# Forgetting attention: weights by values as two passes of rounded operands and rests, the dense group cut in halves between them

## The reference, cut to what matters

```python
def attend(q_blk, c_blk, q_pos):
    s = jnp.einsum('bqhd,bkhd->bhqk', q_blk, k)
    s = s + c_blk[..., None] - c[:, :, None, :]
    s = jnp.where(q_pos[:, None] >= key_pos[None, :], s, -jnp.inf)
    p = jax.nn.softmax(s, axis=-1)
    return jnp.einsum('bhqk,bkhd->bqhd', p.astype(v.dtype), v)
...
o = o * jax.nn.sigmoid(o_gate)
return o @ w_out
```

## Time and profile before

| | us |
|---|---|
| median of 3 runs | 2766.43 |
| lowest and highest of them | 2764.67, 2767.55 |
| the profiled execution | 2765.52 |
| its span, first to last instruction | 2763.8 |
| TensorE busy in the span | 2699.0 (98%) |
| VectorE busy | 1820.4 (66%) |
| ScalarE busy | 1366.1 (49%) |

### The profile page before, as it was taken

How to read it: one execution, slowest core, us unless ns; L and a number is a source line. 1 busy time by engine, 2 the same in 40 slices (tenths; PEclk the granted TensorE clock), 3 DMA queues, 4 the chain that set the end, 5 groups by cost and what they waited for, 6 DMA issues and landing times.

```text
span 2763.8 us, 50228 instructions
## 1 busy us (share of the span) xinstructions
PE 2699.0 (98%) x18315; PEld 2455.7 (89%) x18315; DVE 1820.4 (66%) x2928; ACT 1366.1 (49%) x2401; POOL 307.5 (11%) x269
## 2 busy tenths in 40 slices
PE   7999999999989999899999999999999999899998
PEld 6898899999989999899988888887899988699986
DVE  6777757886367766678853453553677775588832
ACT  4455445664245554556642223232488884455632
POOL 2000011330022121023201011010000000000000
PEclk9999999999999999999999999999999999999999
DMA  4232226884331111268833222223312222223332
GB/s 127 69 76 58 60 75 131 175 181 106 92 97 54 53 53 46 80 144 178 169 105 113 84 72 83 87 68 88 92 54 61 61 61 84 76 85 106 108 94 73
DMA packets 458590, 254.24 MB, mean 92 GB/s; under 512 B 9222, under 2 KB 452871, under 8 KB 458359
## 3 DMA queue, kind: packets, MB, share of 16 engines
q1 hardware_dynamic: 414550, 211.45, 27.0%
q0 software_dynamic: 43152, 38.63, 7.7%
q10 hardware_dynamic: 784, 2.75, 0.3%
HBM read 250.67 MB, written 2.13 MB: 91 GB/s over the span
## 4 chain that ended last, share of the span: by engine, by line
PE 55%; DVE 6%; DMA 4%; issue 3%; ACT 2%; POOL 1%; POOLq 0%; DVEq 0%; ACTq 0%
PE ps L525 24%; PE ps L529 14%; PE ps L919 7%; PE ps L1110 2%; DMA w_sum1a<-in_ffn_w_gate 2%; DMA w_sum1b<-in_ffn_w_gate 2%; PE ps L1268 2%; PE ps L1309 1%; DVE wl L492 1%; PE ps L1298 1%; PE ps L1330 1%; PE ps L1235 1%; PE ps L1155 1%; PE ps L1221 0%; ACT wh L488 0%
## 5 line engine op out<-in xcount | busy, mean ns | idle before, releaser
L492 DVE TENSOR_TENSOR wl<-raw,wh 128x1024 fp32r<-128x1024 f32 (+3 forms) x312 | 370.6, 1188 | 298.3 <-ACT wh L488 295.6
L488 ACT ACTIVATE wh<-raw 128x1024 fp32r<-128x1024 f32 (+3 forms) x312 | 307.0, 986 | 386.5 <-PE ps L525 217.3
L529 PE MATMUL ps<-xh,wh 128*128 128x264 f32 x1872 | 393.6, 291 | 11.3 <-DVE xl L559 6.7
L529 PE MATMUL ps<-xl,wh 128*128 128x264 f32 x1872 | 381.9, 285 | 0.0
L529 PE MATMUL ps<-xh,wl 128*128 128x264 f32 x1872 | 381.6, 285 | 0.0
L529 PEld LDWEIGHTS ps<-xh,wh 128*128 128x128 f32 x1872 | 292.5, 189 | 20.8 <-issue 10.5
L529 PEld LDWEIGHTS ps<-xl,wh 128*128 128x128 f32 x1872 | 291.5, 189 | 0.0
L529 PEld LDWEIGHTS ps<-xh,wl 128*128 128x128 f32 x1872 | 290.6, 189 | 0.0
L525 PE MATMUL ps<-xh,wh 128*128 128x512 f32 x528 | 213.5, 404 | 2.3 <-DVE wl L492 2.3
L525 PE MATMUL ps<-xl,wh 128*128 128x512 f32 x528 | 208.9, 396 | 0.0
L525 PE MATMUL ps<-xh,wl 128*128 128x512 f32 x528 | 207.7, 393 | 0.0
(11 more groups left out here) (453 smaller groups left out, 6603.0 us busy)
## 6 DMA issues: line engine op xcount, KB each, us to landing
raw<-in_w_in SPq DMA_DIRECT2D x88, 512.0 KB, 3.9
raw<-in_ffn_w_gate SPq DMA_DIRECT2D x44, 512.0 KB, 5.6
raw<-in_ffn_w_up SPq DMA_DIRECT2D x44, 512.0 KB, 5.0
raw<-in_w_ffn_in SPq DMA_DIRECT2D x44, 512.0 KB, 3.8
raw<-in_fox_w_in SPq DMA_DIRECT2D x33, 512.0 KB, 4.2
raw<-in_hgrn_w_in SPq DMA_DIRECT2D x32, 512.0 KB, 4.0
raw<-in_ffn_w_down SPq DMA_DIRECT2D x32, 448.0 KB, 3.7
raw<-in_ffn_w_up POOLq DMA_DIRECT2D x36, 256.0 KB, 6.9
```

The lines of the kernel that those rows point to most:

```text
L488: nc.scalar.activation(wh[:, v % 2, 0:nk, :], raw[:, v % RAW_SLOTS, 0:nk, :], ACT.Copy).then_inc(s("w_hi"), 1)
L492: nc.vector.tensor_tensor(wl[:, v % 2, 0:nk, :], raw[:, v % RAW_SLOTS, 0:nk, :], wh[:, v % 2, 0:nk, :].bitcast(F32), ALU.subtract).then_in ...
L529: last = nc.tensor.matmul(ps[:, bank + b, 0:HALF], w[:, slot, kk, :], x[:, k0 + k, b * HALF:(b + 1) * HALF], start=first, stop=end_)
```

## The change

`fox_out` works on fp32r operands. The values become `v_p`: for each head 64 columns rounded and 64 columns of rests side by side, so that one stationary tile of 128 columns holds both (the rounded part first for head 0, the rest first for head 1). The weights become `p_h` (rounded) and `p_l` (rests), and every strip is streamed twice, once from each. So the half of bank 5 where the rounded values stand receives their product and the other half that of the rests, and the two halves have to be added afterwards: ACT copies the other half into `o_t` (`shift`), DVE adds the own half to it (`add_halves`), and the same for the 16 last tokens (`shift_tails`, `add_tails`).

The parts are made by both engines: ACT copies the rounded values and all strips of the rounded weights out of PSUM, DVE subtracts them from PSUM for the rests (`value_rest`, `weight_rest`). The banks may be written again only when DVE is done with them too, so `scores` of head 0 now also waits for `value_rest`. Dense group 3 is cut in two: its first half stays between `turned(0)` and `fox_out(0)`, its second goes behind `turned(1)`. `fox_sums` is cut in two: the queries' sums stand before the second half, the keys' sums behind `fox_out(1)`. The gate's logits, its exponential and its reciprocal move behind with group 3. In the last pair the same value and weight work runs, and the dense work between is as before.

```diff
-    p_t = a.take("p_t", [P, N_STRIP])
-    v_t = a.take("v_t", [P, NTT, P])
+    p_h = a.take("p_h", [P, N_STRIP], F32R)
+    v_p = a.take("v_p", [P, NTT, 4, FOX_D], F32R)
...
+    p_l = a.take("p_l", [P, N_STRIP], F32R)
...
         def fox_out(i, b):
-            pe.wait_ge(s("pt_a"), 2 * i + b + 1)
-            pe.wait_ge(s("pt_b"), 2 * i + b + 1)
-            lo, hi = FOX_D * b, FOX_D * (b + 1)
-            causal_pv(lambda t: ps[lo:hi, 5, t:SEQ], ps[lo:hi, 4, 496:512],
-                      lambda j, k: v_t[0:k, j, lo:hi], p_t, FOX_D).then_inc(s("o_mm"), 1)
+
+            for n, (p, ready) in enumerate(((p_h, "pv_act"), (p_l, "pv_dve"))):
+                pe.wait_ge(s(ready), 10 * i + 4 * b + 4)
+                if b and not n:
+                    pe.wait_ge(s("pv_dve"), 10 * i + 5)
+                for j in range(NFULL):
+                    nc.tensor.matmul(ps[:, 5, P * j:SEQ], v_p[:, j, 2 * b:2 * b + 2, :].rearrange("p b n -> p (b n)"),
+                                     p[:, STRIP0[j]:STRIP0[j] + SEQ - P * j], start=(n + j == 0), stop=(n == 1 and j == NFULL - 1))
...
-            pe.wait_ge(s("vt_ready"), i + 1)
+            pe.wait_ge(s("pv_act"), 10 * i + 1)
+            pe.wait_ge(s("pv_dve"), 10 * i + 1)
             pe.wait_ge(s("o_done"), i + 1)
...
             turned(0)
             if ahead_:
-                pe_group(pe, PH_FOX, i, 3, xh, xl)
+                pe_group(pe, PH_FOX, i, 3, xh, xl, part=0)
...
             turned(1)
             if ahead_:
-                pe.wait_ge(s("psum_free"), evacuated(PH_FOX, i, 3))
-                fox_sums(i + 1)
+                pe.wait_ge(s("psum_free"), evacuated(PH_FOX, i, 2))
+                fox_sums(i + 1, 0)
+                pe_group(pe, PH_FOX, i, 3, xh, xl, part=1)
             else:
                 out_tiles(0, 6, 7)
             fox_out(i, 1)
+            if ahead_:
+                pe.wait_ge(s("psum_free"), evacuated(PH_FOX, i, 3))
+                fox_sums(i + 1, 1)
...
+            def value_rest():
+                dve.wait_ge(s("pv_act"), 10 * i + 1)
+                V.tensor_tensor(v_p[:, 0:NFULL, 1:3, :], ps[:, 2, :].rearrange("p (j b n) -> p j b n", j=NFULL, b=2),
+                                v_p[:, 0:NFULL, 0:4:3, :].bitcast(F32), ALU.subtract)
...
+            def weight_rest(b):
+                for n in range(2):
+                    dve.wait_ge(s("pv_act"), 10 * i + 4 * b + n + 2)
+                    V.tensor_tensor(p_l[:, 512 * n:512 * (n + 1)], ps[:, 2 + n, :], p_h[:, 512 * n:512 * (n + 1)].bitcast(F32),
+                                    ALU.subtract).then_inc(s("pv_dve"), 1)
...
             if ahead_:
                 split_ahead(dve, dve_lo, PH_FOX, i, 0)
+                value_rest()
...
                 scaled_out(PH_FOX, i, 2, v_s[:, :])
-                evacuate(0)
+                weight_rest(0)
                 split_ahead(dve, dve_lo, PH_FOX, i, 3)
-                scaled_out(PH_FOX, i, 3, g_s[:, :])
...
-            gate()
-            evacuate(1)
+                gate()
+            add_halves(0)
+            weight_rest(1)
             if ahead_:
                 qk_scaled(i + 1, 0)
+                scaled_out(PH_FOX, i, 3, g_s[:, :])
                 query_parts(i + 1)
+                gate()
+            add_halves(1)
+            add_tails()
+            if ahead_:
                 qk_scaled(i + 1, 1)
```

More of the change, by code:

```diff
@@ L845, in _ @@
         sp.wait_ge(s("stored"), 16 * NFULL)
[L848 to L857, removed]
     def transposes(src, bank, rows_=P):
@@ L965, in feed_forward, with fox_sums @@
             dense(down, *hidden, ("hid_ready", FT * n))
[L968 to L975, removed]
+        def fox_sums(n, j):
+            pe.wait_ge(s("qn_sq"), 2 * n + j + 1)
+            for b in range(2):
+                last = nc.tensor.matmul(ps[:, FOX_BANKS[j] + b, 0:HALF], mean_64, sq[:, j, b * HALF:(b + 1) * HALF],
+                                        start=True, stop=True)
+            last.then_inc(s("qn_sum"), 1)
         def scores(i, b):
@@ L1008, in fox_out @@
         def fox_out(i, b):
-            pe.wait_ge(s("pt_a"), 2 * i + b + 1)
-            pe.wait_ge(s("pt_b"), 2 * i + b + 1)
-            lo, hi = FOX_D * b, FOX_D * (b + 1)
-            causal_pv(lambda t: ps[lo:hi, 5, t:SEQ], ps[lo:hi, 4, 496:512],
-                      lambda j, k: v_t[0:k, j, lo:hi], p_t, FOX_D).then_inc(s("o_mm"), 1)
+            for n, (p, ready) in enumerate(((p_h, "pv_act"), (p_l, "pv_dve"))):
[5 more added lines that the diff above has]
+                                     p[:, STRIP0[j]:STRIP0[j] + SEQ - P * j], start=(n + j == 0), stop=(n == 1 and j == NFULL - 1))
+            for n, p in enumerate((p_h, p_l)):
+                for j in range(NTT):
+                    k = TOK[j]
+                    last = nc.tensor.matmul(ps[:, 4, tail_out(b)], v_p[0:k, j, 2 * b:2 * b + 2, :].rearrange("p b n -> p (b n)"),
+                                            p[0:k, tail_at(j):tail_at(j) + TAIL], start=(n + j == 0), stop=(n == 1 and j == NFULL))
+            last.then_inc(s("o_mm"), 1)
         def pair_(i, ahead_):
@@ L1073, in _ @@
         pe.wait_ge(s("psum_free"), evacuated(PH_FOXP, 0, 3))
-        fox_sums(0)
+        for j in range(2):
+            fox_sums(0, j)
         loop(pe, PH_FOX.n, lambda i: pair_(i, True))
@@ L1718, in qk_square, with qk_rsqrt @@
             nc.scalar.activation(sq[:, j, :], qk_raw[:, j, :], ACT.Square).then_inc(s("qn_sq"), 1)
-        def qk_rsqrt(n):
-            for j in range(2):
-                act.wait_ge(s("qn_sum"), 2 * n + j + 1)
-                act.wait_ge(s("qn_done"), 2 * n + j + 1)
-                rt_j = two(post_t[:, j, :])
-                act_rsqrt(act, pair(FOX_BANKS[j]), rt_j, rt_j, eps, "qn_ln", 2 * n + j).then_inc(s("qn_r"), 1)
+        def qk_rsqrt(n, j):
+            act.wait_ge(s("qn_sum"), 2 * n + j + 1)
+            act.wait_ge(s("qn_done"), 2 * n + j + 1)
+            rt_j = two(post_t[:, j, :])
+            act_rsqrt(act, pair(FOX_BANKS[j]), rt_j, rt_j, eps, "qn_ln", 2 * n + j).then_inc(s("qn_r"), 1)
         def key_parts(n):
@@ L1747, in _ @@
         split_ahead(act, act_hi, PH_FOXP, 0, 3)
-        qk_rsqrt(0)
+        for j in range(2):
+            qk_rsqrt(0, j)
         key_parts(0)
@@ L1790, in pair_ @@
                 split_ahead(act, act_hi, PH_FOX, i, 3)
-                gate(PH_FOX, i, 3)
             else:
                 gate(PH_FOXG, 0, 0)
+            shift(0)
             evacuate(1)
             if ahead_:
-                qk_rsqrt(i + 1)
+                qk_rsqrt(i + 1, 0)
+                gate(PH_FOX, i, 3)
+            shift(1)
+            shift_tails()
+            if ahead_:
+                qk_rsqrt(i + 1, 1)
                 key_parts(i + 1)
```

52 lines of the change are left out of this document (39 added, 13 removed).

## The result

The changed kernel takes 2830.4 us (median of four runs, 2830.3 to 2834.0), the kernel before 2765.8 us in the runs beside it. The ratio is 1.0236, with a 95% interval of 1.0223 to 1.0248: 64.6 us slower. The prediction was 2812 us with a range of 2796 to 2824. Its sign and its mechanism hold, but its size is some 18 us short, and the time lies outside the range.

The account below looks back on a forecast made before the run. PE was taken as the bound, with 0.66 us of slack in DVE's list. Profiled 2765.5 plus 33 (waits), 12 (clock), 2.1 (first pair) and 0.5 (last pair) made 2813; 2812 us was given, range 2796 to 2824.

Parts of the forecast that it names:

- the list on DVE: DVE's work from group 3's end to the next scores: 15.56 us, against 9.87 us of PE's work meanwhile.
- the clock's term in the loop: Granted clock falls behind each pair's wait: 3.4 us at half clock cost 1.7 us, 12 us for seven waits.
- the last pair: Two cheaper products (-1.1) against some 1.6 us of uncovered rests before `fox_out(1)`: +0.5 us, between -1 and +2.
- the first pair: Only `wl` and `value_rest` are put before the scores: 1.14 and 0.87, with the handing over 2.1 us.
- tails in it: Ten 16-column tails in `fox_out`: 1.1 us, bounded by 0.73 from below and 1.12 from above.
- scores to group 3's end, without the clock: PE's stretch from a pair's first scores to group 3's end: 28.95 us against 23.85 before, no wait expected.
- wait before the scores: PE idles before each pair's scores, released by DVE's `value_rest`: 5.7 us.
- pair: One pair's scores to the next pair's: 44.5 us against 39.80, with the clock's fall a period of 46 us.
- the clock stays low longer: Rival: low stretch behind a wait lasts up to twice the 3.4 us, 12 us more, 2824 us; chance 0.11.
- the handing over: From the end of `value_rest` on DVE to the scores on PE: 0.05 us.
- The wide strips: Four strips with 1280 columns in `fox_out`, two passes: 1.30 us, against 2.21 before.
- The rival of a faster kernel with PE as the bound: Rival: DVE's list behind group 3 takes no more than PE's 9.87 us, time 2758 us; chance 0.05.

Follow-up runs that it names:

- Experiment 1: Changed kernel with 28 products that nobody reads put on PE before each pair's first scores; 2810.2 us, ratio 1.0169 to the kernel before.
- Experiment 5: Changed kernel with group 3 whole, the gate and both sums back in their old places, the two-pass product kept; 2804.9 us, ratio 1.0143 to the kernel before.
- Experiment 8: Two-pass product in a rebuilt order: group 3 whole, value rests first, gate on ScalarE, gated output in the next pair; 2770.8 us, ratio 1.0014 to the kernel before.
- experiment 4: Changed kernel with the gate's addition and reciprocal taken off DVE, made on ScalarE by logarithm and exponential; 2804.8 us, ratio 1.0144 to the kernel before.
- experiment 3: Changed kernel with the value rests ahead of the weights' split on DVE; 2822.0 us, ratio 1.0207 to the kernel before.
- experiment 2: Changed kernel with 14 products that nobody reads before each pair's scores, filling the first half of the wait; 2828.9 us, ratio 1.0223 to the kernel before.
- 6: Kernel before with its plain float32 product, only the order changed: group 3 in halves, sums apart, gate behind the second product; 2778.7 us, ratio 1.0042.
- experiment 9: As experiment 8, but each wide product waits only for its own piece of the weights; 2770.6 us, ratio 1.0012 to the kernel before.
- experiment 7: Changed kernel with each tail of `fox_out` beside a wide product of the same stationary tile; 2831.7 us, ratio 1.0234 to the kernel before.
- the last two kernels: The kernels of experiment 8 and experiment 9, at 2770.8 and 2770.6 us over eleven runs each.

## Why the prediction was wrong, step by step

The mechanism was the forecast one: PE idles before each pair's scores until DVE's list with the moved reciprocal and `value_rest` at its end is through, and the clock falls behind each wait. Nothing of the kind appeared elsewhere in the loop. What failed are sizes. Of the 18 us missing, the list on DVE has 6.5 (0.93 in seven pairs), the clock's term in the loop 5.3 (0.76 in seven), the last pair 5.4 and the first pair 0.5.

| term, us | forecast | measured |
|---|---|---|
| `fox_out` | 2.40 | 2.66 |
| tails in it | 1.1 | 1.43 |
| scores to group 3's end, without the clock | 28.95 | about 29.1 |
| list on DVE, group 3's end to the scores | 15.56 | 16.49 |
| wait before the scores | 5.7 | 6.26 |
| clock, per pair | 1.7 | 2.46 |
| pair | 46.2 | 47.9 |
| first pair | +2.1 | +2.6 |
| last pair and what follows, with the fall of the clock behind its wait | +2.2 | +7.6 |

**The clock's term, mis-sized.** 1.7 us per pair was half of the 3.4 us at the lower level that the earlier trace rows show behind two waits. These are not the same thing twice. Behind the wait of 2.41 us the whole low stretch is 3.4 us long (62.6 to 66.0). Behind that of 6.27 us it is 6.8 us long (789.7 to 796.5), and only what lay behind the wait was read. In the changed kernel each low stretch before scores is 6.8 us long and begins 1.2 to 2.1 us before the work, so 4.7 to 5.6 us of it fall on work. The scores cost 1.95 more and the tiles behind them 0.51, together 2.46. Experiment 1 gives 20 us for the whole against the 12 forecast. The rival "the clock stays low longer" was to bring 12 us more; about 8 of them came. I had given it 0.11, since PE is dense behind the scores. That was no reason: PE is dense here too, and more of the stretch falls on work all the same. The Trainium skill (TensorE: Matmul & The Clock Gate, section "HAM oscillation — how this bites in real kernels") has a loop pay for the fall in every round; the trace agrees, with 0.44 to 0.45 us for the first product behind each of its eight waits, instead of 0.22. Experiment 5, with shorter waits, does not pay in every round.

**The list, mis-sized by 0.93.** Every entry that I had read from the rows of this pair held to 0.1 us: the queries' parts, the gate 3.95 for 3.84, `k_s` to the end of the split 6.95 for 6.85. The adding of halves and tails took 1.11 for 0.9. The largest miss is the last one, the handing over. Between the end of `value_rest` (159.81 + 0.27) and PE's first product (160.52) are 0.44 us; I had put 0.05. It is no effect of the clock: in experiment 5 it is as long in front of scores that run at full clock (152.44 + 0.27 to 153.15).

**The tails.** The bound from above, 1.12 for ten products of that form, was passed: 1.43. I had priced them like short products with other stationary tiles in the earlier trace rows; ten of them in a row with full 128-column tiles take 0.14 each. The wide strips went the other way, 1.23 us for the 1.30 forecast and the 2.21 before. The Trainium skill (TensorE: Matmul & The Clock Gate, section "Weight-path perf modes — Fast Weight Load (FWL) and DoubleRow") has a fast load for 128 weights of a type other than FP32. No run here can tell whether fp32r gets it; the tails took more than the 0.112 us each that the five short products of the earlier trace rows show, not less.

**The ends**, the worst step in proportion. +0.5 was a balance of cheaper products and uncovered rests. The waits behind the rests are there and small. What I left out is that they bring the clock down once more (PE's rows, then the stretch behind):

```profile
419.39 0.82 PE L1008 MATMUL ps<-p_h,v_p 128*128 128x512 f32 x4 [0.84 <-DVE o_t L2756]
420.96 0.99 PE L1008 MATMUL ps<-p_l,v_p 128*128 128x512 f32 x4 [0.75 <-DVE p_l L2749]
```
```profile
421.40:428.20 6.80, 6.80 (x32) 6.70 (x31) 2.32 (x5) 1.59 (x4) 0.00 (x0) 0.51 0.00 0
```

6.8 us at the lower level are 3.4 us lost, of the 5.4 that are missing here. Behind the wait before the last scores the low clock costs 2.5 us and not 1.7: head 0's scores take 4.18 for 2.19, and head 1's, which follow directly in this pair, 2.70 for 2.17. That is 0.8 more. Head 0's product takes 3.08 us (412.85 to 415.93) for the 2.40 forecast, 0.7 more, and head 1's 0.3 more at the 2.66 that it takes in the loop. The last 0.2 us stay open.

**What was right**: that PE stops being the bound, the place of the wait and what ends it, the period's growth by the list, and that the rest of the program keeps its length. The granted clock of the stage was named as near 0.93, and over the seven pairs it is 0.93, but that is luck: the 3.4 low us in 46.2 of the forecast itself would give 0.96. The rival of a faster kernel with PE as the bound needed a list 5.7 us shorter. Experiment 8 has it, and shows that its 2758 was too hopeful too, since the product saves 0.06 to 0.47 us per head and not 0.54.

## What to carry to other kernels

Where PE is the bound by less than a microsecond over another engine's list, ask first what a change adds to or moves into that list; a cheaper product can hardly pay for it. Here it saved 0.28 us per head, while the reciprocal, taken off the list in experiment 4, made the wait 2.7 us shorter. Price a new wait on PE as the wait plus what the products behind it lose at the lower clock, up to the last slowed one, in every round and at the loop's ends too. Shortening the wait doesn't surely give that part back: at 5.1 us (experiment 3) and at 3.7 (experiment 2) nothing of it came back, at 3.5 (experiment 4) 7 us did, and at 1.3 (experiment 1) all 20.

## What the runs showed of the hardware that I had not expected

- Whether the clock falls behind a wait, and for how long, goes by the wait only roughly. The granted clock over the first 8 us of dense work behind waits before scores, from all eleven kernels (1.00 is no fall; 0.79 means 1.7 us lost, 0.67 means 2.6):

| wait, us | experiment, pairs | granted clock over 8 us |
|---|---|---|
| 1.3 to 1.4 | 1, 5, 6: fourteen pairs | 1.00 in all |
| 2.3 to 2.5 | before, 2, 6: first pair; 4, 5: last pair | 0.79, 0.59, 0.79, 0.79, 0.79 |
| 2.8 | 5: four pairs | 1.00, 0.59, 1.00, 0.79 |
| 3.5 | 4: six pairs | 0.79, 0.58, 0.67, 0.79, 0.79, 0.79 |
| 3.5 to 3.7 | 3, 8, 9: first pair | 0.79, 0.59, 0.79 |
| 3.7 | 2: six pairs | 0.63 to 0.69 |
| 4.9 | the changed kernel, 4, 5, 7: first pair | 0.65, 0.79, 0.64, 0.58 |
| 5.1 | 3: six pairs | 0.58 to 0.79 |
| 6.3 | the changed kernel: six pairs | 0.67 to 0.70 |

  The waits not listed fit in: 0.5 and 0.9 us with 1.00, 3.0 us with 0.79, 4.2 us with 0.65, 5.4 us and more with 0.58 to 0.70. So before scores 1.4 us never brought the fall and 3.5 us and more always did; between them it came in all but two cases. Once it comes, the loss lies between 1.7 and 3.4 us and doesn't follow the wait: these low stretches last 3.4 or 6.8 us, once 10.2, and what counts is how much of one falls on work.
- Unchanged code shows the same. Behind the 2.45 us wait at 1138.85 the kernel before keeps a granted clock of 1.00. In experiment 9 the same wait is followed by a slower product, 0.73 for 0.48 us, and a clock of 0.81 over the next 8 us. Its attention stage ends with the kernel before's to 0.2 us, while its profiled execution is 5.6 us longer, and three such places have 4.8 of them. Behind the waits that end at 1139.57, 1155.22 and 2439.57 (2.45, 2.88 and 1.79 us, the same in both kernels to 0.01) the clock is low for 3.4 us in experiment 9 and stays at 1.00 in the kernel before, and the distance between the two traces grows by 1.51, 1.72 and 1.54 us. So here the stage was level with the kernel before's, and the loss was one of the clock in code that the change does not touch. It may also be why single executions of the last two kernels lie up to 8 us apart. The first of the waits and the stretches behind all three:

```profile
1139.57 0.73 PE L1241 MATMUL ps<-yh,wh 128*128 128x264 f32 x2 [2.45 <-DVE yl L2961]
```
```profile
1139.60:1143.60 4.00, 4.00 (x20) 4.00 (x21) 1.18 (x3) 1.27 (x2) 0.00 (x0) 0.57 0.45 131
1156.00:1160.00 4.00, 4.00 (x23) 4.00 (x22) 3.42 (x5) 2.85 (x5) 0.00 (x0) 0.59 0.47 136
2439.60:2443.60 4.00, 4.00 (x11) 3.14 (x12) 4.00 (x6) 1.03 (x2) 0.00 (x0) 0.57 0.44 131
```

- Two waits of 0.84 and 0.75 us in short order, near the end of the attention stage, were followed by 6.8 us at the lower level, though neither is as long as the 1.44 us that cost nothing elsewhere. In experiment 5 one wait of 0.75 us alone was followed by 3.4 us at that level in two of seven pairs.
- A product of 16 columns takes 0.11 to 0.14 us with a stationary tile of 128 columns. A neighbour with the same tile saves no load: the trace has one for each product (experiment 7).
